# Chunked gated recurrence: block copies into A on ScalarE, projections of f and g cut into quarters between the levels

## What is computed

```python
z = einsum('btd,dc->btc', x, w_in)            # hq, hf, hi, g_hg are its last 2048 columns
log_f = logaddexp(log(lb), log1p(-lb) + log_sigmoid(hf)); k = -expm1(log_f)
# in chunks, S the state carried from chunk to chunk:
G = cumsum(log_f); decay = exp(G[t] - G[s])   for s <= t
A = einsum('bthd,bshd,btshd->bhts', q, k, decay)
o = A @ v + (q * exp(G)) @ S
S = exp(G_last) * S + (k * exp(G_last - G)).T @ v
o = rmsnorm(o) * hg_g * silu(g_hg)
```

## Time and profile before

| | |
|---|---|
| median of 3 runs | 3070.25 us |
| profiled execution, its own time | 3071.02 us |
| its span | 3069.2 us |
| mean granted TensorE clock over the span | 0.94 |
| TensorE busy (matmul) | 2715.5 us, 88% |
| VectorE busy | 1645.2 us, 54% |
| GpSimd busy | 1053.5 us, 34% |
| ScalarE busy | 1012.8 us, 33% |
| hardware DMA queue | 184.90 MB, 17.9% of 16 engines |

### The profile page before, as it was taken

One profiled execution on the slowest core, in us unless ns is written; L12 is line 12 of the kernel. 1 busy time (PEld: TensorE's weight loads), 2 busy tenths in 40 slices (PEclk: granted clock), 3 DMA queues, 4 the chain that ended last, 5 costly groups with the idle time before them and its releaser, 6 DMA issues. The chain is left out here.

```text
span 3069.2 us, 53622 instructions
## 1 busy us (share of the span) xinstructions
PE 2715.5 (88%) x20498; PEld 2212.6 (72%) x20498; DVE 1645.2 (54%) x3207; ACT 1012.8 (33%) x2154; POOL 1053.5 (34%) x940
## 2 busy tenths in 40 slices
PE   6999858989999689999969999579998996799998
PEld 5777647777777568888857777467777775688887
DVE  4566655677666652222236665646767676522222
ACT  3333342444444331111123333424444444311111
POOL 1212112454455443333212221125445454433332
PEclk9999978999999899999979999789999998899999
DMA  4111212000000322222141111310000003221211
GB/s 145 48 41 41 109 54 59 22 21 24 21 21 21 138 81 88 87 85 83 65 159 42 40 41 58 115 53 22 28 21 21 24 21 138 81 67 67 67 67 45
DMA packets 95089, 186.23 MB, mean 61 GB/s; under 512 B 11504, under 2 KB 56560, under 8 KB 92912
## 3 DMA queue, kind: packets, MB, share of 16 engines
q1 hardware_dynamic: 94992, 184.90, 17.9%
HBM read 134.86 MB, written 51.90 MB: 61 GB/s over the span
## 5 line engine op out<-in xcount | busy, mean ns | idle before, releaser
L105 PE MATMUL r_Z<-w_rec_high,w_rec_xh 128*128 128x512 f32 x1088 | 463.2, 426 | 39.1 <-POOL w_rec_xl L945 30.6
L105 PE MATMUL r_Z<-w_rec_low,w_rec_xh 128*128 128x512 f32 x1088 | 441.6, 406 | 0.0
L105 PE MATMUL r_Z<-w_rec_high,w_rec_xl 128*128 128x512 f32 x1088 | 440.3, 405 | 0.0
L105 PE MATMUL a_Z<-w_attn_high,w_attn_xh 128*128 128x512 f32 (+1 forms) x816 | 303.1, 371 | 0.0
L105 PE MATMUL a_Z<-w_attn_low,w_attn_xh 128*128 128x512 f32 (+1 forms) x816 | 291.8, 358 | 0.0
L105 PE MATMUL a_Z<-w_attn_high,w_attn_xl 128*128 128x512 f32 (+1 forms) x816 | 290.9, 357 | 0.0
L954 POOL TENSOR_TENSOR r_qE<-r_qT,r_E 128x256 f32<-128x256 f32 x230 | 184.0, 800 | 293.1 <-ACT r_E L1040 158.7
L105 PEld LDWEIGHTS r_Z<-w_rec_high,w_rec_xh 128*128 128x128 f32 x1088 | 218.2, 201 | 84.0 <-issue 40.6
L105 PEld LDWEIGHTS r_Z<-w_rec_high,w_rec_xl 128*128 128x128 f32 x1088 | 215.0, 198 | 49.4
L105 PEld LDWEIGHTS r_Z<-w_rec_low,w_rec_xh 128*128 128x128 f32 x1088 | 217.9, 200 | 41.6
L1040 ACT ACTIVATE r_E<-r_E 128x512 f32<-128x512 f32 x230 | 145.0, 631 | 250.6 <-DVE r_E L1176 250.6
(11 more groups left out here) (258 smaller groups left out, 5714.6 us busy)
## 6 DMA issues: line engine op xcount, KB each, us to landing
w_attn_xraw<-dram_xT SPq DMA_DIRECT2D x34, 512.0 KB, 3.5
r_xraw<-dram_xT SPq DMA_DIRECT2D x34, 512.0 KB, 3.2
o_mraw<-dram_mixT SPq DMA_DIRECT2D x34, 512.0 KB, 4.5
dram_y_all<-o_hb SPq DMA_DIRECT2D x34, 512.0 KB, 2.9
w_rec_whole<-dram_w_in SPq DMA_DIRECT2D x16, 1024.0 KB, 12.4
w_attn_whole<-dram_w_in SPq DMA_DIRECT2D x16, 640.0 KB, 7.9
dram_mixT<-a_mixT SPq DMA_DIRECT2D x136, 64.0 KB, 2.1
dram_mixT<-r_u SPq DMA_DIRECT2D x34, 256.0 KB, 2.0
```

What stands on the lines that cost most here:

```text
L105: mm = pe.matmul(out, a[:, c, :], b[:, c, :], start=(first and c == chunks[0] and a is xh and b is wh), stop=(last and c == chunks[-1] and ...
```

## The change

Three things change, in `recurrence_phase`:

- The four copies of `near` into the diagonal blocks of A leave VectorE's `take_near` and become ScalarE's `gather(n)`, with the same wait for `near_done` and the same increment of `A_done`. In ScalarE's program it stands behind `front_log(n+1)` and ahead of `copy_khT(n)`; for tile 0 right behind `middle(0)`.
- TensorE's `step(n)` projects f and g of the next tile in quarters (two chunks, 6 matmuls each) and puts one level between any two of them. Level 0 follows q and the first quarter of f; v stays whole. ScalarE's `copy_z(n+1)` moves from behind level 4 to behind level 3 accordingly. Tile 1's order on TensorE, written out apart, stays.
- ScalarE's `copy_z(1)` moves from behind level 2 of the samples' tile to behind its ends and `gather(0)`.

```diff
--- before.py
+++ after.py
@@ -1053,6 +1053,13 @@
                     act.activation(used, used, ACT.Exp)
                     act.activation(qG[:, :, :], G[:, :, :], ACT.Exp).then_inc(S["ends_exp"], 1)
 
+                def gather(n):
+
+                    act.wait_ge(S["near_done"], n + 1)
+                    for r in range(0, P, NEAR):
+                        op = act.activation(A[r:r + NEAR, :, r:r + NEAR], near[r:r + NEAR, :, :], ACT.Copy)
+                    op.then_inc(S["A_done"], 1)
+
                 def copy_khT(n):
                     act.wait_ge(S["khT_ps"], n + 1)
                     wait(act, S["update_ps"], n)
@@ -1086,10 +1093,10 @@
                 def around_first(l):
                     if l == 0:
                         split_high(2, 0)
-                    if l == 2:
-                        copy_z(1)
 
                 middle(0, DEC_LEVELS, around_first)
+                gather(0)
+                copy_z(1)
                 copy_khT(0)
                 front_log(1)
                 front_exp(1)
@@ -1103,11 +1110,12 @@
                     def after(l):
                         if l == 1 and not last:
                             split_high(n + 2, k)
-                        if l == 4:
+                        if l == 3:
                             copy_z(n + 1)
 
                     middle(n, LEVELS, after)
                     front_log(n + 1)
+                    gather(n)
                     copy_khT(n)
                     front_exp(n + 1)
                     squares(n)
@@ -1200,10 +1209,6 @@
                     wait_apart(dve, S["dve_passed"], S["diag_ps"], n + 1)
                     dve.copy_predicated(near[:, :, :], C["diagonal"][:, :].unsqueeze(1).to_broadcast([P, GH, NEAR]),
                                         M[:, 0:GH * NEAR].rearrange("p (g t) -> p g t", g=GH)).then_inc(S["near_done"], 1)
-                    dve.wait_ge(S["near_done"], n + 1)
-                    for r in range(0, P, NEAR):
-                        op = dve.tensor_copy(A[r:r + NEAR, :, r:r + NEAR], near[r:r + NEAR, :, :])
-                    op.then_inc(S["A_done"], 1)
 
                 def middle(n, k, levels):
                     dve.wait_ge(S["sum_done"], n + 1)
@@ -1413,22 +1418,27 @@
                 transpose_qf(0)
 
                 def step(n, k):
-                    project(n + 1, 1 - k, "q")
+                    later = (n + 1, 1 - k)
+                    project(*later, "q")
+                    project(*later, "f", 0, 2)
                     level(n, 0, LEVELS[0])
+                    project(*later, "f", 2, 4)
                     level(n, 1, LEVELS[1])
-                    if not (isinstance(n, int) and n == 0):
-                        transpose_u(n - 1)
-                    project(n + 1, 1 - k, "f")
-                    for l in (2, 3):
-                        level(n, l, LEVELS[l])
+                    project(*later, "f", 4, 6)
+                    transpose_u(n - 1)
+                    level(n, 2, LEVELS[2])
+                    project(*later, "f", 6, KC)
+                    level(n, 3, LEVELS[3])
+                    project(*later, "g", 0, 2)
                     transpose_qf(n + 1)
-                    project(n + 1, 1 - k, "g", 0, KC // 2)
+                    project(*later, "g", 2, 4)
                     level(n, 4, LEVELS[4])
-                    project(n + 1, 1 - k, "g", KC // 2, KC)
-                    for l in (5, 6):
-                        level(n, l, LEVELS[l])
+                    project(*later, "g", 4, 6)
+                    level(n, 5, LEVELS[5])
+                    project(*later, "g", 6, KC)
+                    level(n, 6, LEVELS[6])
                     diagonal(n)
-                    project(n + 1, 1 - k, "v")
+                    project(*later, "v")
                     transpose_kh(n)
                     output_and_update(n)
```

## The result

The changed kernel takes **2936.76 us**, the median of 4 runs (2933.05 to 2938.76), where the kernel before took 3070.25 us: a ratio of 0.9565, 95% interval 0.9535 to 0.9596. (A fourth run of the kernel before, of 7090.86 us, is left out of it.) The profiled execution took 2933.05 us, its span 2931.3; that is 137.9 us off the span of before. The forecast was 2937 us.

What follows compares the result with a forecast made beforehand. It took TensorE's waits for level products and the slow clock behind them, in 35 to 36 us recurrence steps, as the bound. 121.8 us from the steps plus 12.2 from the sample tile, 134 off 3071.0, gave 2937 us; range 2918 to 2960.

Steps and rivals of the forecast that it cites:

- The recurrence's steps: Both layers' steady tiles: 13 steps of 31.2 us and a last 37.2 make 442.8 against 508.6 and 498.8, saving 121.8.
- TensorE's own tile: TensorE's work in one recurrence tile without waits or slow clock: about 30.4 us, 31.2 with the added breaks.
- four breaks: Extra cuts in TensorE's projections of f and g: 0.2 us each, 0.8 a tile; bounds 0.1 to 0.4 each.
- The front: VectorE's operations behind front_log start 2.2 us earlier; level 0's product has 1.1 us in hand instead of 2.3 late.
- T: Start of ScalarE's front_log, from which the prediction counts times up to level 0's product.
- the port conflict: VectorE's bounds tensor_scalars would wait for a late GpSimd low half of x, up to 2.4 us; 0.6 to spare.
- the first rival: Level chain or shared port keeps part of the gain: 2968 us, or 2984 with both; chance 0.2.
- The level chain: Products for levels 4 to 6 ready at 17.0 and 21.3 us into the step, wanted at 17.7 and 21.9.
- the walk: The prediction's timing of one step from the start of q, through f, level products and front_log, to level 0.
- ScalarE's copies: Four copies into A at 0.27 us each, 1.1 a tile, covered before the output matmuls, so costing nothing.
- The sample's tile: TensorE's 4.10 us wait before kh's transposes goes, plus 2 us of slow clock: 6.1 a layer, 12.2 us.
- The slower rival: Projections in eight 1.4 us bursts hold TensorE's clock down: 250 us more than forecast, 3187 us; chance 0.04.

Runs made afterwards that it cites:

- experiment 6: Changed kernel with three breaks (projection cuts with a level put in) fewer: 2922.82 us, rerun 2914.24; with one break more, diagonal in the middle of v: 2946.31 us.
- experiment 7: Changed kernel with the first operation of VectorE's front run once more into a spare tile: 2960.3 us; three times more: 3057.44 us.
- experiment 2: Kernel before with f and g by quarters and copy_z(n + 1) behind level 3, copies staying on VectorE: 2983.04 us, ratio 0.9703.
- experiment 5: Changed kernel with each of ScalarE's four copies also made once more into an unread spare tile: 2936.92 us, ratio 0.9528.
- Experiment 3: Kernel before with only the sample tile's first copy of q and f moved behind its ends: 3070.88 us, ratio 0.9989.
- experiment 1: Kernel before with only the four copies into A moved from VectorE to ScalarE's gather: 2976.88 us, ratio 0.9682.
- experiment 4: Kernel before with GpSimd's low half of x moved between levels 3 and 4, copies staying on VectorE: 2980.22 us, ratio 0.9695.
- the best version: Changed kernel with three breaks fewer, levels 0 and 1, 2 and 3, 5 and 6 together: 2914.24 us, against 2935.44 for the changed kernel.

## Why the prediction was right, step by step

**The recurrence's steps** were to save 121.8 us and saved 127.8. The step is 30.98 instead of the 31.2 forecast. TensorE's own tile was put at 30.4 and four breaks at 0.2 each. By experiment 6 a break is about 0.24, so with four of them the tile without them is about 30.0: the 30.4 was 0.4 too high, and the four breaks, at 0.8, were 0.16 too low. The forecast's 0.2 was read from 12 matmuls up to the start of the next level, and leaves out the way back: a projection starts 0.38 us behind level 5 (737.08 to 737.46), the diagonal only 0.28 behind level 6. The 30.4 is 34.01 less its waits, and a wait costs more than its bracket says: the two of experiment 7 are 0.70 in their brackets and 0.85 in the step. With three waits in that tile this makes some 0.2 of the 0.4, an estimate; the rest is open. The two errors leave 0.22 a step, and 26 x 0.22 = 5.7 of the 6.0 us are this.

**The front** came as walked: `lsig` at T+3.25 (forecast 3.2), level 0's product at T+15.23 (15.2), front_log 21.78 into the step (21.9), 1.0 us in hand (1.1). The overlap of `lsig` with the low half cost nothing, as was taken. Between the low half's end (T+4.27, forecast 4.9) and the bounds' operations (T+5.55, forecast 5.5) there are 1.3 us in hand, twice the forecast's 0.6, so the port conflict of the first rival stayed away.

**The level chain** too: the copy of q and f starts at 13.65 (forecast 13.5), level 4's product ends at 16.7 (17.0), level 6's at 21.2 (21.3), and TensorE takes level 6 at 21.67 (21.9). What the walk left out is level 2, the tightest of all with 0.47 us. It did no harm here, but the prediction said "level 0 has 1.1 us in hand", and the runs show level 2 waiting first (experiment 6, the break in v, where level 0 does not wait) or with it (experiments 2 and 7). 1.25 us more on the chain is enough to bring waits of the first rival's kind about, at some 23.5 us in all (2960.3 - 2936.76, not measured beside each other).

**ScalarE's copies** were put at 0.27 each and take 0.30; covered, and covered at twice the number (experiment 5).

**The sample's tile** was to give 12.2 us: the stretch from the first load to level 0 of tile 1 shrank by 6.9 and 5.8 us, 12.7. Experiment 3 gives 5.5 + 5.1 of that to this part. The rest, 2.1 us, isn't resolved; the copies' move also touches those tiles. TensorE is not dense up to level 0 of tile 1, as the prediction took it to be (4.11 us of idle ahead of it). The gain comes through all the same: this idle begins behind TensorE's own last transposes there (L1492) and moves with them. TensorE's timeline of the changed kernel, the end of f, the transposes of `kh`, the output and g:

```profile
459.67 0.40 PE L105 MATMUL r_Z<-w_rec_high,w_rec_xl 128*128 128x512 f32 x1
459.90 0.60 PE L1393 MATMUL r_M<-ident,r_kh 128*128 128x128 f32 x4
460.34 1.00 PE L1477 MATMUL r_O<-r_A,r_v 128*128 128x64 f32 x8
461.15 0.48 PE L105 MATMUL r_Z<-w_rec_high,w_rec_xh 128*128 128x512 f32 x1
```

The 4.10 us of the earlier trace rows are gone, and nothing takes their place.

**The clock** was taken as full where no wait is over half a microsecond, and is. Waits of 0.2 to 0.9 us in every step, single ones up to 1.2 (experiments 1, 2, 4 and 7), left it at 1.00, and those of 2.3 us (before) and 2.8 us (experiment 7) bring it down in some steps. What lies between 1.2 and 2.3 us wasn't run. The slower rival (bursts of 1.4 us hold the clock down) did not come: a projection cut eight times runs at 1.00, if no cut turns into a long wait. The Trainium skill, TensorE: Matmul & The Clock Gate, section A second HAM failure mode, describes short idles between groups of matmuls that make the clock go up and down. The runs show this at 2.3 and 2.8 us, and do not show it at 0.3 to 1.2 us.

In sum, 127.8 + 12.7 = 140.5 us, and step 1 gives 0.6 more. The span shows 137.9: 2.2 us go the other way ahead of the first recurrence phase (its first load is at 398.05 instead of 395.86), which the change doesn't touch, and 1.0 elsewhere. So the mechanism was right and its sizes close, but that the median meets the forecast within 0.3 us is luck: the parts gave 7 us more than the 134 forecast, 3.2 of that were lost outside them, and the profiled execution is itself 3.7 us below the median.

What the prediction didn't ask is which part earns what. It added up the copies' 2.2 us and the later level 0 as two needs, and experiments 1 and 2 show that either is enough for about two thirds of the gain. And the quarters bought room with breaks, of which experiment 6 takes three back.

## What to carry to other kernels

When a wait of some microseconds in a dense matmul stream brings down the clock behind it, the first remedy that shortens it to under about a microsecond takes most of the gain; count the clock's part once, not once for each remedy. Here it stayed up with waits of up to 1.2 us, and with waits of 2.3 us it fell in most steps. Before moving an operation because it is long, look at what runs beside it on the other engine of its port: moving the neighbour did as much for the step as moving the copies. Cut a matmul stream only as often as the products' due times ask: each cut cost about 0.25 us, and levels that are ready together can be issued together. Before moving a small group of matmuls, look at what another engine does with its result: the diagonal's move held up VectorE's next front.

## What the runs showed that was not expected

- A wait can hide in the weight loads: the kernel with a break in v has no wait on a matmul, yet level 2's weights wait up to 0.30 us for GpSimd's product, and the step is 0.35 us longer where the break alone gives 0.26.
- Waits of one length (2.82 to 2.83 us) leave the clock in different states: the level behind takes 0.64, 0.89 or 1.07 us. The kernel before, with waits of 2.3 us, spreads over 17 us (3073.88 to 3090.81, nine runs on one chip), the changed one over 5 (2933.04 to 2938.48, five runs on the same chip); but the best version, without such waits, also spreads over 9 (2909.7 to 2919.11), so that the waits are the cause of the spread isn't shown. A small gain in the kernel before has to be read from the stretch that it touches.
- Level 2, not level 0, has the least in hand in the changed kernel (0.47 against 1.0 us), with level 6 next to it (0.49).
